# Three rounded passes for the 512-column products of an HGRN projection

## What is computed

```python
h  = modulate(x, norm_g, shift, scale)          # RMS norm, (1 + scale), shift
hc = modulate(ctx, norm_g, shift_c, scale_c)
q, v, zf, zb, gate = split(h @ w_in, 5)         # w_in: 1024 x 10240; the same for hc
q  = silu(q)
f  = lb + (1 - lb) * sigmoid(z);  g = log(f);  k = 1 - f      # forward with zf, backward with zb
# per head (16 of 128 channels), forward and, on reversed time, backward:
S_t = diag(exp(g_t)) S_(t-1) + k_t^T v_t;  o_t = S_t^T q_t    # S starts from the context's last state
y  = (rmsnorm(o_f + o_b) * silu(gate)) @ w_out;  x = x + gate_ada * y
```

## Time and profile before

| | |
|---|---|
| median of 3 runs | 4398.36 us (4397.22 to 4402.07) |
| the profiled execution | 4401.36 us, span 4399.6 us |
| TensorE busy | 3939.0 us, 90% of the span |
| VectorE, ScalarE, GpSimd busy | 1793.3, 1239.6, 576.4 us |
| moved by DMA | 313.48 MB, mean 71 GB/s |

### The profile page before, as it was taken

One profiled execution on the slowest core, in us unless ns is written; L12 is line 12 of the kernel. 1 busy time (PEld: TensorE's weight loads), 2 busy tenths in 40 slices (PEclk: granted clock), 3 DMA queues, 4 the chain that ended last, 5 costly groups with the idle time before them and its releaser, 6 DMA issues. The chain is left out here.

```text
span 4399.6 us, 58371 instructions
## 1 busy us (share of the span) xinstructions
PE 3939.0 (90%) x24027; PEld 2612.3 (59%) x24027; DVE 1793.3 (41%) x2975; ACT 1239.6 (28%) x2170; POOL 576.4 (13%) x302
## 2 busy tenths in 40 slices
PE   5899999999689998977899999999687767899998
PEld 2566667666554444435455555788546547687876
DVE  1243445434419884113223323533227447334421
ACT  1333344333312212123212322422322131323321
POOL 0000000000210000001000002444420020343442
PEclk7999999999799997988989999999898898999999
DMA  7211111110245545011402113333110110332331
GB/s 263 63 40 43 48 43 38 43 43 24 58 115 162 160 156 172 19 54 39 89 11 58 43 36 103 86 96 96 34 41 3 31 29 3 82 96 82 95 91 62
DMA packets 509547, 313.48 MB, mean 71 GB/s; under 512 B 28748, under 2 KB 491141, under 8 KB 509350
## 3 DMA queue, kind: packets, MB, share of 16 engines
q1 hardware_dynamic: 509350, 310.68, 24.3%
HBM read 308.54 MB, written 2.10 MB: 71 GB/s over the span
## 5 line engine op out<-in xcount | busy, mean ns | idle before, releaser
L552 PE MATMUL hg_bank<-hT,hg_w 128*128 128x512 f32 x1024 | 447.3, 592 | 0.0
L1081 PE MATMUL cv_bank<-hT,cv_w 128*128 128x512 f32 x768 | 340.5, 599 | 13.7 <-DMA cv_w<-in_conv_w_in_dram 13.7
L552 PEld LDWEIGHTS hg_bank<-hT,hg_w 128*128 128x128 f32 x1024 | 193.3, 190 | 223.6 <-issue 221.9
L1196 DVE SCALAR_TENSOR_TENSOR conv_u<-cv_pad,vec,conv_u 128x512 f32<-128x512 f32 x480 | 319.2, 745 | 0.0
L2942 POOL TENSOR_TENSOR tl_wl<-tl_w,tl_wh 128x1024 fp32r<-128x1024 f32 (+1 forms) x104 | 246.7, 2374 | 521.6 <-ACT tl_wh L3053 521.5
L1081 PEld LDWEIGHTS cv_bank<-hT,cv_w 128*128 128x128 f32 x768 | 145.1, 192 | 188.3 <-issue 173.8
L1994 POOL TENSOR_TENSOR mp_wl<-mp_w,mp_wh 128x1024 fp32r<-128x1024 f32 x72 | 173.5, 2411 | 599.9 <-ACT mp_wh L2074 599.9
L3053 ACT ACTIVATE tl_wh<-tl_w 128x1024 fp32r<-128x1024 f32 (+1 forms) x104 | 108.5, 1043 | 357.4 <-PE tl_bank L2979 354.8
L2977 PE MATMUL tl_bank<-tl_room,tl_wh 128*128 128x512 f32 x464 | 188.4, 406 | 13.0 <-POOL tl_wl L2942 12.1
L2979 PE MATMUL tl_bank<-tl_room,tl_wl 128*128 128x512 f32 x464 | 182.6, 394 | 0.0
L2978 PE MATMUL tl_bank<-tl_room,tl_wh 128*128 128x512 f32 x464 | 181.0, 390 | 0.0
(11 more groups left out here) (669 smaller groups left out, 7815.2 us busy)
## 6 DMA issues: line engine op xcount, KB each, us to landing
cv_ada<-in_w_ada_dram SPq DMA_DIRECT2D x48, 1024.0 KB, 7.5
hg_w<-in_hgrn_w_in_dram SPq DMA_DIRECT2D x80, 512.0 KB, 3.8
mp_w<-in_w_mlp_dram SPq DMA_DIRECT2D x64, 512.0 KB, 4.1
ada_w<-in_ada_w_dram SPq DMA_DIRECT2D x12, 2048.0 KB, 19.8
cv_w<-in_conv_w_in_dram SPq DMA_DIRECT2D x48, 512.0 KB, 4.0
tl_w<-in_w_ffn_in_dram SPq DMA_DIRECT2D x44, 512.0 KB, 4.0
at_w<-in_w_in_dram SPq DMA_DIRECT2D x24, 512.0 KB, 4.0
tl_w<-in_w_in_dram SPq DMA_DIRECT2D x20, 512.0 KB, 3.9
```

Source lines behind the costliest of these rows:

```text
L552: ins = pe.matmul(bank[:, 0:w], W[m][:, k, :], src[:, k, 0:w], start=(k == 0), stop=(k == KD - 1))
L1081: ins = pe.matmul(ps[n % RING][:, :], W[n % SLOTS][:, k * P:(k + 1) * P], K.hT[:, k, :], start=(k == 0), stop=(k == KD - 1))
L1196: ins = dve.scalar_tensor_tensor(o, x, by, o, ALU.mult, ALU.add)
```

## The change

- The 512-column groups ZF, ZB, Q and G are made as three rounded passes. V's groups and the context groups stay as they are and read the raw weights.
- h is rounded once (hh, by ScalarE) and subtracted (hl, by VectorE) at the start of the stage.
- Each weight tile is rounded by ScalarE (`weights_high`) and its low half made by VectorE (`weights_low`), at set places of their programs. There are two slots of halves: ZF and Q share one, ZB and G the other.
- To make room, G's weights share V's buffer, sigmoids go straight into f1, a few small tiles are laid over others, and hh takes the place of xT: the residual stream is stored to DRAM at the end of the modulation stage (2 MB) and loaded back when the last projection is done.
- The last two heads are written out behind ScalarE's and VectorE's loops.

```diff
+    with ExitStack() as under:
+        K.hgH = K.sb(under, "hg_hh", [P, KD, T], F32R)
     K.xT = K.sb(K.ctx, "xT", [P, KD, T])
+    K.spill = nc.dram_tensor("x_spill", [P, KD * T], F32, kind="Internal").ap()
     K.hT = K.sb(K.ctx, "hT", [P, KD, T])
...
+                sp.dma_start(K.spill, K.xT[:, :, :].rearrange("p k t -> p (k t)")).then_inc(spilled, 16)
+                sp.wait_ge(spilled, 16)
...
-        W = [K.sb(st, f"hg_w{m}", [P, KD, P]) for m in range(5)]
+        W = [K.sb(st, f"hg_w{m}", [P, KD, P]) for m in range(4)]
+        W.append(W[V])
+        WH = [K.sb(st, f"hg_wh{m}", [P, KD, P], F32R) for m in range(2)]
+        WL = [K.sb(st, f"hg_wl{m}", [P, KD, P], F32R) for m in range(2)]
+        hh = K.hgH
+        hl = K.sb(st, "hg_hl", [P, KD, T], F32R)
         vt = [K.sb(st, f"hg_v{i}", [P, NT // P, P]) for i in range(2)]
-        sg = [[K.sb(st, f"hg_sig{i}{d}", [P, NT]) for d in range(2)] for i in range(2)]
+        f1 = [K.sb(st, f"hg_f{d}", [P, NT]) for d in range(2)]
         qs = [K.sb(st, f"hg_q{i}", [P, T]) for i in range(2)]
         gs = [K.sb(st, f"hg_gate{i}", [P, T]) for i in range(2)]
-        f1 = [K.sb(st, f"hg_f{d}", [P, NT]) for d in range(2)]
...
-        osq = K.sb(st, "hg_osq", [P, T])
+        osq = ATS[:, :, :].rearrange("q c t -> q (c t)")
...
-                def load(h, first, shift=0):
-                    at = h * P if first else sp.snap(h * P)
-                    for m in (V, ZF, ZB, Q, G):
-                        if not first:
+                def load(m, at):
+                    sp.dma_start(W[m][:, :, :], wv[:, :, at]).then_inc(w_in[m], 16)
+
+                for m in (V, ZF, ZB, Q):
+                    load(m, slice(COL[m], COL[m] + P))
+                sp.wait_ge(proj, LAST_OF[V])
+                load(G, slice(COL[G], COL[G] + P))
+                with sp.Fori(0, NH - 1) as h:
+                    at = sp.snap(h * P)
+                    for m in (ZF, Q, ZB, V, G):
+                        if m in (ZF, ZB):
                             sp.wait_ge(proj, NG * h + LAST_OF[m])
-                        sp.dma_start(W[m][:, :, :], wv[:, :, bass.ds(at + (COL[m] + shift), P)]).then_inc(w_in[m], 16)
-                load(0, True)
-                with sp.Fori(0, NH - 1) as before:
-                    load(before, False, P)
+                        elif m == Q:
+                            sp.wait_ge(low, 4 * h + 3)
+                        elif m == V:
+                            sp.wait_ge(low, 4 * h + 4)
+                        else:
+                            sp.wait_ge(proj, NG * h + (NG + LAST_OF[V]))
+                        load(m, bass.ds(at + (COL[m] + P), P))
+                sp.wait_ge(proj, NG * NH)
+                sp.dma_start(K.xT[:, :, :].rearrange("p k t -> p (k t)"), K.spill).then_inc(x_back, 16)
+                sp.wait_ge(x_back, 16)
...
-                        if c == 0:
+                        if m == V and c == 0:
                             pe.wait_ge(w_in[m], 16 * h + 16)
+                        elif c == 0:
+                            pe.wait_ge(low, 4 * h + m)
+                        if n == 2 and first:
+                            pe.wait_ge(h_low, KD)
                         if n >= 4 or not first:
                             pe.wait_ge(evac, NG * h + (n - 3))
                         src, w = (cT, TC) if c else (hT, T)
@@ -547,10 +573,16 @@
                                                     start=(k == 0), stop=(k == KD - 1))
                                 if owed is not None and c == 0 and t == 1:
                                     mean_square(owed)
-                        else:
+                        elif c == 1:
                             for k in range(KD):
                                 ins = pe.matmul(bank[:, 0:w], W[m][:, k, :], src[:, k, 0:w],
                                                 start=(k == 0), stop=(k == KD - 1))
+                        else:
+                            wh, wl = WH[(m - 1) % 2], WL[(m - 1) % 2]
+                            for k in range(KD):
+                                pe.matmul(bank[:, :], wh[:, k, :], hh[:, k, :], start=(k == 0), stop=False)
+                                pe.matmul(bank[:, :], wh[:, k, :], hl[:, k, :], start=False, stop=False)
+                                ins = pe.matmul(bank[:, :], wl[:, k, :], hh[:, k, :], start=False, stop=(k == KD - 1))
...
+                def weights_high(m, h, freed):
+                    act.wait_ge(w_in[m], 16 * h + 16)
+                    if freed is not None:
+                        act.wait_ge(proj, freed)
+                    act.activation(WH[(m - 1) % 2][:, :, :], W[m][:, :, :], ACT.Copy).then_inc(high, 1)
+
+                def evacuate(h, p, groups, first=False):
                     for n in groups:
                         m, c = GROUPS[n]
                         act.wait_ge(proj, NG * h + (n + 1))
+                        if n == 2 and not first:
+                            act.wait_ge(k_ok, 2 * h)
...
-                            s = sg[p][m - ZF]
+                            s = f1[m - ZF]
...
+                def rest(h, p, first=False, last=False):
+                    weights_high(Q, h, NG * h + 3)
+                    evacuate(h, p, (2, 3, 4), first)
+                    weights_high(G, h, NG * h + 5)
+                    evacuate(h, p, (5, 6))
+                    if not last:
+                        weights_high(ZF, h + 1, NG * h + 7)
+                    evacuate(h, p, (7,))
+                    if not last:
+                        weights_high(ZB, h + 1, NG * h + 8)
+
+                def step(h, p, last=False):
 
                     logs(h - 1)
                     exps(h - 1, 0)
                     evacuate(h, p, range(0, 2))
                     exps(h - 1, 1)
-                    evacuate(h, p, range(2, NG))
+                    rest(h, p, last=last)
                     recur(h - 1)
 
-                evacuate(0, 0, range(NG))
+                weights_high(ZF, 0, None)
+                for k in range(KD):
+                    act.activation(hh[:, k, :], hT[:, k, :], ACT.Copy).then_inc(h_high, 1)
+                weights_high(ZB, 0, None)
+                evacuate(0, 0, (0, 1))
+                rest(0, 0, first=True)
                 step(1, 1)
-                with act.Fori(1, NH // 2) as j:
+                with act.Fori(1, NH // 2 - 1) as j:
                     step(2 * j, 0)
                     step(2 * j + 1, 1)
+                step(NH - 2, 0)
+                step(NH - 1, 1, last=True)
...
+                def weights_low(m, h):
+                    dve.wait_ge(high, 4 * h + m)
+                    dve.tensor_tensor(WL[(m - 1) % 2][:, :, :], W[m][:, :, :], WH[(m - 1) % 2][:, :, :].bitcast(F32), ALU.subtract).then_inc(low, 1)
...
+                for k in range(KD):
+                    dve.wait_ge(h_high, k + 1)
+                    dve.tensor_tensor(hl[:, k, :], hT[:, k, :], hh[:, k, :].bitcast(F32), ALU.subtract).then_inc(h_low, 1)
+                for h, m in ((0, ZF), (0, ZB), (0, Q), (0, G), (1, ZF), (1, ZB)):
+                    weights_low(m, h)
...
-                def prepare(h, p):
+                def prepare(h, p, left):
                     for d in range(2):
                         dve.wait_ge(evac, NG * h + 4 + 2 * d)
-                        dve.tensor_scalar(f1[d][:, :], sg[p][d][:, :], omlb[:, bass.ds(h + NH * d, 1)], TINY,
+                        dve.tensor_scalar(f1[d][:, :], f1[d][:, :], omlb[:, bass.ds(h + NH * d, 1)], TINY,
                                           ALU.mult, ALU.max).then_inc(f_ok, 1)
                     for d in range(2):
...
+                        if left >= 1:
+                            weights_low(Q if d == 0 else G, h + 1)
+                    if left >= 2:
+                        weights_low(ZF, h + 2)
+
+                def recur(h, p, left):
                     for d in range(2):
                         dve.wait_ge(sc_ok, 2 * h + (d + 1))
...
+                    if left >= 2:
+                        weights_low(ZB, h + 2)
                     dve.wait_ge(rs_ok, h + 1)
...
-                with dve.Fori(0, NH // 2) as j:
+                with dve.Fori(0, NH // 2 - 1) as j:
                     for p in range(2):
-                        prepare(2 * j + p, p)
-                        recur(2 * j + p, p)
+                        prepare(2 * j + p, p, 2)
+                        recur(2 * j + p, p, 2)
+                for p in range(2):
+                    prepare(NH - 2 + p, p, 1 - p)
+                    recur(NH - 2 + p, p, 1 - p)
 
 
 def mat(w, rhs, kt=KD, col=0, step=P, pieces=((0, 0, P),)):
```

More of the change, by code:

```diff
@@ L276, in modulation_phase @@
         w_in = sems[0:SLOTS]
-        summed, copied, turned, biased, zeroed, ready = sems[SLOTS:SLOTS + 6]
+        summed, copied, turned, biased, zeroed, ready, spilled = sems[SLOTS:SLOTS + 7]
         with nc.Block() as block:
@@ L480, in hgrn_phase @@
         omlb = K.sb(st, "hg_omlb", [P, 32])
```

(23 more changed lines are left out.)

1 line of the change is left out of this document (removed).

## The result

| | before | after |
|---|---|---|
| time, median of 4 runs each on the same chip | 4397.79 us (4396.92 to 4402.07) | 4337.52 us (4332.97 to 4340.39) |
| profiled execution, span | 4401.36, 4399.6 | 4336.56, 4334.6 |
| ratio after/before, 95% interval | | 0.986 (0.9845 to 0.9875) |

Faster, as predicted, but by 60.3 us where 90 were forecast, and 11.5 us above the upper end of the range. The forecast for the profiled execution was a span of 4309.3, so 25 us are missing there.

What follows compares the result with a forecast made beforehand. TensorE's instruction stream in the hgrn stage was taken as the bound. From 4401.4 us, 91.5 came off for products and 1.2 was added for the store: 4311.1 profiled, 4308 for the median, range 4301 to 4326.

Steps and rivals of the forecast that it cites:

- The failing step: Hgrn stage: TensorE, busy 99% of 939 us, is the bound; shortening its stream counts until another engine is late.
- the sum: Whole kernel: 4401.4 less 91.5 for the products plus 1.2 for the store gives 4311.1 us profiled, 4308 for the median.
- The lower end of my range: Whole kernel: 4301 us, the forecast's lower end and 3 us for clock edges that fall elsewhere.
- None of the rivals: Four alternatives: small waits per head 0.14; late low halves, slow clock 0.02; passes not cheaper 0.01; store sharing with load 0.04.
- Rival 2: Hgrn heads: low halves come too late and TensorE's clock falls; 4436 us if G's is 4 us late; chance 0.02.
- The sign named for a wrong forecast: TensorE in the hgrn stage: a granted clock below 1.00, one of several signs listed as showing the forecast wrong.
- its counterpart: TensorE in the hgrn stage: busy 98% or more at clock 1.00 would show the forecast right.
- The products: ZF, ZB, Q, G groups: rounded passes every 0.2265 us, 1.43 us saved per group, 91.5 us over 64 groups.
- the row of the last stage: Last stage's rounded products: issued every 0.229 us, giving 1.37 us saved per group, 87.7 us in all.
- The operands: Each hgrn head: rounded weights and low halves arrive before TensorE needs them, VectorE's subtraction taking 1.2 us; no wait.
- the tightest slack: ZB's first product in each head: ScalarE's copy of V done at 20.27, due at 20.57, slack 0.3 us or more.
- The spill: End of modulation: 2 MB store ends at 103.5 to 105.8, costing 0 to 2 us, taken as 1.2; load back hidden.

Runs made afterwards that it cites:

- a_unroll: The changed kernel with TensorE's loop over head pairs written out, nothing else touched: 4310.80 us, ratio 0.9801 to the kernel before.
- a_g_unroll: The changed kernel with G's products left at full f32 and TensorE's loop written out: 4336.33 us, ratio 0.986 to the kernel before.
- b_split1: The kernel before with only ZF's 256-column context group cut into two 128-column halves, loop body 1739 records: 4433.67 us, ratio 1.0068.
- b_split2: The kernel before with the context groups of ZF and ZB cut into two 128-column halves, loop body 1803 records: 4436.05 us, ratio 1.0086.
- a_fewer: The changed kernel with the first head pair written out and three iterations of two pairs, two returns instead of six: 4314.80 us, ratio 0.981.
- b_split_half: The kernel before with ZF's context group cut into two halves in odd heads only, loop body 1707 records: 4400.02 us, ratio 1.0003.

## Why the prediction was wrong

- **The failing step.** "TensorE's own instruction stream is the bound, and whatever shortens it counts until another engine is late". I priced the stream by the duration of its instructions and charged nothing for their number: the sum has no term for the return to the head of TensorE's loop, which is to put it at 0. The change shortens the time of each group and lengthens the loop's body by 134 records, from 1675, which is kept between iterations, to 1809, which is not. What the runs showed in its place: 6 returns at 5.2 us, 3.3 of stop and 1.9 of slow clock, so 31 us in the profiled execution, and 27 to 31 us by a_unroll and by a_g_unroll. The lower end of my range held 3 us for "clock edges that fall elsewhere"; the real edges cost 1.5 to 3.0 us at each return, the other way.
- **None of the rivals was this one.** Rival 2 had its mechanism in half: idle time, then half clock. But it looked for the idle time in late data. The sign named for a wrong forecast, a granted clock below 1.00, came true: 0.99 over the stage, 0.50 after each stop. So did its counterpart: TensorE is busy 97% of the stage, not 98% or more; in a_unroll it is 99%.
- **What could have been read beforehand.** The profile of before lists 145 instruction transfers for the program and none within an iteration of this loop: the body was being kept. The Trainium skill, Runtime: NRT & Kernel Launch, "Instruction fetch mechanics", says that TensorE holds 2048 instructions, refilled in blocks of 256, and that a taken branch whose target is not in the current window of two pages stalls until the page is fetched. The trace agrees on the block, 255 records to a transfer, and on the stall, a taken branch of 3.31 to 3.70 us with a transfer 1.0 us into it. It agrees with neither size: by the 2048 instructions 1809 would still fit, and 1739 did not; by two pages not even 1675 would, and it is kept. Counted in blocks, the page's figure comes closer, as an estimate: 1707 records touch seven or eight blocks of 256 depending on where they begin, and the two kernels of that length came out differently. That the number of blocks decides was not shown: 1675 and 1739 records too touch seven or eight.
- **The products: right, by the slower row.** Three passes are issued every 0.229 us (24 products of a group but for the first), forecast 0.2265; that is the row of the last stage in the earlier trace rows, which I had put aside for the range. A group saves 1.37, not 1.43, so the 64 groups 87.7 instead of 91.5: 3.8 us of the miss. ZF took 600.74 - 595.16 = 5.58 (5.44 forecast), its first product 0.1 longer, and the context group 3.26 (3.45). A head takes 55.87 us without the loop, forecast 55.7 (61.34 before, inside a body). a_unroll is 87.9 under the kernel before of its comparison, forecast 90.3; its 4310.8 is 2.8 above the predicted 4308.
- **The operands: right.** VectorE's subtraction took 1.22 (1.2). Both V copies were done at 603.84 and ZB began at 604.00, so the tightest slack was 0.16, forecast 0.3. No wait on a low half, none in the first head, where ZF starts at 149.41.
- **The spill: right in kind.** 0 against 1.2: the store had landed at 102.3, ahead of the 103.5 that I gave as the least and of the stage's last operation. The load back had landed at 1039.2, before the wait of the earlier trace rows, which now begins at 1048.7.

## What to carry over

Where an engine at its limit runs a hardware loop, count the instructions in its body before and after, not their time alone, and look in the DMA view for instruction transfers inside one iteration of the old kernel: none means, as far as these runs go, that the body is kept, and growth may meet a cliff. The sign behind the cliff is an "issue" wait at the head of the loop, once per iteration, with a branch of some 3 us in it and mostly a slow clock after it. The cure can be one line: written out, this loop gives 4310.8 us in place of 4337.5, the best kernel of this study; in the old kernel the same line is worth nothing.

## What the hardware showed that I had not expected

- A return to a body that isn't kept is recorded as a long branch: 3.3 to 3.7 us in after (up to 5.0 in b_split1), 0.2 where the body is kept. Behind it the granted clock is mostly 0.50 for some 3 us, but not always: after idle times of 3.22 us in b_split2 and of 3.15 in a_fewer it stayed at 1.00.
- The limit is a step: b_split1, 64 records over the old body, loses as much by the median (36 us) as b_split2 with 128 more (37 us); b_split_half, with 32 more, loses nothing, until its body is moved by 96 records and it loses 26. Where exactly the limit lies, and by what rule the place counts, stays open.
- Instruction transfers in a straight line cost nothing here: a_unroll has 8 of them in a stretch as long as an iteration and no stop.
- GpSimd's 128x1024 subtraction takes 2.35 us alone. Beside VectorE's products of two tiles it takes 6.0: it ends 2.2 us after the last of these, while VectorE keeps its pace. The Trainium skill, SBUF — State Buffer, "SBUF: two separate sides", describes the port pair that the two share as an exclusive lock, held for a whole instruction, with the other side fully blocked. The runs agree with the block. Here GpSimd alone paid: in the gaps between VectorE's products, which follow one another without a pause, it did not come in.
